# Delta-rule inverses on packed 32x32 diagonal blocks, masks in one operation, out projection begun on the other branches' rows

## The reference

```python
lower = jnp.where(strict, jnp.einsum('bhncd,bhnsd->bhncs', kb, k) * decay, 0.0)
eye = jnp.eye(cs, dtype=jnp.float32)
tinv = lax.linalg.triangular_solve(lower + eye, jnp.broadcast_to(eye, lower.shape),
                                   left_side=True, lower=True, unit_diagonal=True)
...
mix = jnp.concatenate([y_a, y_b, y_c], axis=-1) @ p['w_out'][l]
x = x + g1 * mix
```

## Time and profile before

| | us |
|---|---|
| median of 3 runs (2239.47 to 2243.78) | 2240.41 |
| profiled execution | 2252.45 |
| its span | 2250.3 |

### The profile page before, as it was taken

One profiled execution on the slowest core, in us unless ns is written; L12 is line 12 of the kernel. 1 busy time (PEld: TensorE's weight loads), 2 busy tenths in 40 slices (PEclk: granted clock), 3 DMA queues, 4 the chain that ended last, 5 costly groups with the idle time before them and its releaser, 6 DMA issues.

```text
span 2250.3 us, 35703 instructions
## 1 busy us (share of the span) xinstructions
PE 2027.0 (90%) x13488; PEld 1770.6 (79%) x13488; DVE 1040.9 (46%) x1950; ACT 689.9 (31%) x1394; POOL 189.5 (8%) x246
## 2 busy tenths in 40 slices
PE   4999988989799999997999879998299999999993
PEld 3777776887699999996778768875289989989782
DVE  2297254551433323332795645513372753827534
ACT  2110323330422112213112333303252643626422
POOL 1000002430000000001000023300100000000001
PEclk8999887999899999998998889998699999999995
DMA  8444269101222222313331200020667868869673
GB/s 294 162 173 176 97 262 420 67 21 60 70 84 92 84 68 84 102 58 120 129 131 50 75 1 1 8 73 0 233 189 240 315 203 286 280 229 326 190 252 126
DMA packets 87062, 328.10 MB, mean 146 GB/s; under 512 B 9666, under 2 KB 10274, under 8 KB 85634
## 3 DMA queue, kind: packets, MB, share of 16 engines
q1 hardware_dynamic: 78850, 295.17, 37.9%
q0 software_dynamic: 5120, 20.43, 2.4%
q10 hardware_dynamic: 2944, 10.49, 1.3%
HBM read 276.59 MB, written 49.46 MB: 145 GB/s over the span
## 4 chain that ended last, share of the span: by engine, by line
PE 85%; DVE 6%; DMA 3%; ACT 3%; issue 2%; POOL 1%; SPq 0%; ACTq 0%; POOLq 0%; DVEq 0%
PE PB L964 11%; PE PB L965 11%; PE PB L781 9%; PE PB L783 9%; PE PB L782 9%; PE PB L919 7%; PE PB L916 6%; PE PB L917 3%; PE PB L596 3%; PE PB L434 2%; PE PB L612 2%; PE PB L611 2%; PE PB L522 1%; PE PB L1015 1%; PE PB L957 1%
## 5 line engine op out<-in xcount | busy, mean ns | idle before, releaser
L964 PE MATMUL PB<-hT,ring 128*128 128x288 f32 x1024 | 343.2, 418 | 22.2 <-DVE hT L2020 12.2
L965 PE MATMUL PB<-hT,ring 128*128 128x288 f32 x1024 | 338.6, 413 | 0.0
L964 PEld LDWEIGHTS PB<-hT,ring 128*128 128x128 f32 x1024 | 196.6, 195 | 78.8 <-issue 19.8
L965 PEld LDWEIGHTS PB<-hT,ring 128*128 128x128 f32 x1024 | 198.9, 194 | 56.0
L781 PE MATMUL PB<-HH,VH 128*128 128x288 f32 x704 | 209.8, 298 | 17.2 <-DVE HL L1774 15.9
L916 PE MATMUL PB<-XX,UH 128*128 128x512 f32 (+3 forms) x704 | 213.0, 370 | 1.8 <-DVEq L1866 1.5
L782 PE MATMUL PB<-HL,VH 128*128 128x288 f32 x704 | 208.9, 297 | 0.0
L783 PE MATMUL PB<-HH,VL 128*128 128x288 f32 x704 | 208.2, 296 | 0.0
L917 PE MATMUL PB<-XX,UL 128*128 128x256 f32 (+3 forms) x704 | 181.6, 258 | 0.0
L781 PEld LDWEIGHTS PB<-HH,VH 128*128 128x128 f32 x704 | 133.2, 189 | 17.8 <-issue 17.8
L916 PEld LDWEIGHTS PB<-XX,UH 128*128 128x128 f32 x704 | 132.1, 188 | 13.3 <-DVEq L1866 1.9
(11 more groups left out here) (435 smaller groups left out, 3712.6 us busy)
## 6 DMA issues: line engine op xcount, KB each, us to landing
SS<-in_w_ada SPq DMA_DIRECT2D x88, 512.0 KB, 5.7
ring<-in_moe_gu SPq DMA_DIRECT2D x88, 512.0 KB, 4.6
RX<-in_moe_gu SPq DMA_DIRECT2D x88, 512.0 KB, 4.6
ring<-in_w_in SPq DMA_DIRECT2D x48, 512.0 KB, 3.5
ring<-in_ffn_gu SPq DMA_DIRECT2D x46, 512.0 KB, 3.4
RX<-in_moe_dn SPq DMA_DIRECT2D x44, 512.0 KB, 4.5
ring<-in_moe_dn SPq DMA_DIRECT2D x44, 512.0 KB, 4.5
moe_in<-CO SPq DMA_DIRECT2D x1, 15360.0 KB, 49.8
```

Of the source, the lines that this page charges most:

```text
L964: mm(PM[b][:, 0:HN], w, hT[:, k, 0:HN], start=(k == 0), stop=(k == KD - 1))
L965: end = mm(PS[b][:, 0:HN], w, hT[:, k, HN:T], start=(k == 0), stop=(k == KD - 1))
```

## The change

The five levels within blocks of 32 are done on the diagonal 32x32 blocks alone. ScalarE packs the four diagonal blocks of `UU` into `UC` (`diagonal_blocks`), VectorE masks them for all levels in one operation (`all_masks`), and GpSimd's `level_mask` is gone. `power` and `merged` issue 32x32 products, block `j` on rows and columns 32j of TensorE's array, for four heads after one wait; the three sets of chunks have a PSUM bank each. Level 5 joins blocks of 32 and level 6 those of 64, through full matrices `T64` and `TF` that GpSimd clears beforehand and into which ScalarE spreads the small blocks (`level_blocks`). The normalisation of chunks 0, 1 and 4 is shared out over later levels, and their turns move to level 5, level 6 and the tail. The first two tiles of the out projection are begun on rows 0, 1, 6 and 7 of `hT` in the tail, and finished on rows 2 to 5 where the projection stood. Two helper semaphores and eight small copies at the program's start, which cut the masks to 32 columns, complete it.

```diff
+Q = 32
+QLEVELS = 5
...
+        TC = [a.rearrange("p (a h c) -> p a h c", a=2, h=H) for a in (wk(7)[:, 0:256], wk(9)[:, 0:256], xaf[:, 640:896])]
...
+        LVQ = CO[:, C_LVL + QLEVELS * P:C_LVL + QLEVELS * P + QLEVELS * Q].rearrange("p (v c) -> p v c", c=Q)
+        IDQ = CO[:, C_LVL + QLEVELS * P + QLEVELS * Q:C_LVL + QLEVELS * P + (QLEVELS + 1) * Q]
+        quad = lambda j: slice(j * Q, (j + 1) * Q)
...
-        BANK_P, BANK_T, BANK_SM = (6, 4), (7, 0), (3, 2)
+        BANK_INV, BANK_SM = (6, 7, 5), (3, 2)
...
             def power(n, v):
...
+                m, b = chunk(n)[1], buf(n)
                 if v == 0:
...
+                    pe.wait_ge(S["um_ready"], prep(l, n))
                 else:
...
+                    pe.wait_ge(S["t_done"], inv(l, n, v - 1) + 1)
+                if v < QLEVELS:
+                    for hh in range(H):
+                        for j in range(m // Q):
+                            end = mm(p_out(n)[quad(j), hh, :], UM[b][quad(j), v, hh, :], IDQ[quad(j), :] if v == 0 else TC[b][quad(j), 0, hh, :],
+                                     start=True, stop=True, tile_position=(j * Q, j * Q))
+                elif v == QLEVELS:
+                    for hh in range(H):
+                        for j in (0, 2):
+                            end = mm(p_out(n)[quad(j + 1), hh, :], UU[b][quad(j), hh, (j + 1) * Q:(j + 2) * Q], TC[b][quad(j), 0, hh, :],
+                                     start=True, stop=True, tile_position=(j * Q, (j + 1) * Q))
+                else:
+                    pe.wait_ge(S["t64_ready"], full(l, n) + 1)
+                    for hh in range(H):
+                        end = mm(p64_out(n)[:, hh, :], UU[b][0:P // 2, hh, P // 2:P], T64[b][0:P // 2, hh, :],
+                                 start=True, stop=True, tile_position=(0, P // 2))
+                end.then_inc(S["p_pe"], 1)
             def merged(n, v):
...
+                m, b = chunk(n)[1], buf(n)
+                pe.wait_ge(S["p_copied"], merge(l, n, v) + 1)
+                t, pc = TC[b], PD[b]
+                for hh in range(H):
+                    if v < QLEVELS:
+                        for j in range(m // Q):
+                            mm(t_out(n)[quad(j), 0, hh, :], t[quad(j), 1, hh, :], pc[quad(j), hh, :], start=True, stop=True, tile_position=(j * Q, j * Q))
+                            end = mm(t_out(n)[quad(j), 1, hh, :], pc[quad(j), hh, :], t[quad(j), 1, hh, :], start=True, stop=True, tile_position=(j * Q, j * Q))
+                    elif v == QLEVELS:
+                        mm(t_out(n)[quad(1), 0, hh, :], t[quad(1), 1, hh, :], pc[quad(1), hh, :], start=True, stop=True, tile_position=(Q, Q))
+                        for j in (0, 2):
+                            end = mm(t_out(n)[quad(j), 1, hh, :], pc[quad(j + 1), hh, :], t[quad(j + 1), 1, hh, :],
+                                     start=True, stop=True, tile_position=((j + 1) * Q, j * Q))
+                    else:
+                        end = mm(t64_out(n)[:, hh, :], PC64[b][P // 2:P, hh, :], TF[b][P // 2:P, hh, P // 2:P], start=True, stop=True, tile_position=(P // 2, 0))
+                end.then_inc(S["t_pe"], 1)
             def t_final(n, last):
-                pe.wait_ge(S["t_done"], 2 * inv(l, n, last) + 2)
+                pe.wait_ge(S["t_done"], inv(l, n, last) + 1)
...
-                    end = mm(bank4(2, m)[:, hh, :], inv_tt(n, hh)[0:m, 0:m], VB[buf(n)][0:m, hh, :], start=True, stop=True)
+                    if n == 4:
+                        for j in range(m // Q):
+                            end = mm(out[quad(j), hh, :], TC[b][quad(j), 1, hh, :], v[quad(j), hh, :], start=True, stop=True, tile_position=(j * Q, j * Q))
+                    else:
+                        end = mm(out[:, hh, :], TF[b][:, hh, :], v[:, hh, :], start=True, stop=True)
...
-                if v == 2:
+                if v == 5:
                     back_to_features(0)
-                if v == 3:
+                if v == 6:
                     pe.wait_ge(S["yb_ready"], normed(l, 0))
                     back_to_features(1)
-                if v == 4:
-                    pe.wait_ge(S["yb_ready"], normed(l, 1))
-                    back_to_features(4)
...
             k_state(3)
+            pe.wait_ge(S["yb_ready"], normed(l, 1))
+            back_to_features(4)
             pe.wait_ge(S["r_ready"], stated(l, 3))
             t_final(3, LEVELS - 1)
             pe.wait_ge(S["vn_copied"], scan(l, 2))
...
             outputs(3, 0)
             new_state(3)
             outputs(3, 1)
+            pe.wait_ge(S["ya_ready"], 2 * (l + 1))
+            pe.wait_ge(S["yc_ready"], 2 * (l + 1))
+            pe.wait_ge(S["t_done"], len(INV) * (l + 1))
+            out_begun(0)
             pe.wait_ge(S["yb_ready"], normed(l, 4))
             back_to_features(2)
+            pe.wait_ge(S["o_copied"], NCH * (l + 1))
+            out_begun(1)
             pe.wait_ge(S["yb_ready"], normed(l, 2))
             back_to_features(3)
...
+            def out_part(l, s, rows):
+                for k in rows:
+                    w = ring[:, slot_of(FILL["out", l], s), k * P:(k + 1) * P]
+                    mm(PM[s][:, 0:HN], w, hT[:, k, 0:HN], start=(k == OTHER[0]), stop=(k == DELTA[-1]))
+                    end = mm(PS[s][:, 0:HN], w, hT[:, k, HN:T], start=(k == OTHER[0]), stop=(k == DELTA[-1]))
+                return end
...
+                if stage == "out":
+                    for s in range(2):
+                        out_part(l, s, DELTA).then_inc(S["w_used"], 1)
+                    for s in range(2, 4):
+                        wait_landed(pe, f0, s, 0)
+                        wait_free(s % 2, (t0 + s) // 2)
+                        tile_mms(slot_of(f0, s), s % 2)
...
+                def out_begun(s):
+                    wait_landed(pe, FILL["out", l], s, 0)
+                    wait_free(s, (TILE["out", l] + s) // 2)
+                    out_part(l, s, OTHER)
+                mixer_pe(pe, l, z_tile, out_begun)
...
+            def diagonal_blocks(n):
+                act.wait_ge(S["uu_ready"], prep(l, n))
+                for j in range(chunk(n)[1] // Q):
+                    e = fn(UC[buf(n)][quad(j)], UU[buf(n)][quad(j), :, j * Q:(j + 1) * Q], ACT.Copy)
+                e.then_inc(S["uuc_ready"], 1)
+            def level_blocks(n):
+                b = buf(n)
+                act.wait_ge(S["pad_ready"], 4 * l + 1)
+                act.wait_ge(S["t_done"], inv(l, n, QLEVELS - 1) + 1)
+                for j in range(P // Q):
+                    c = slice(j * Q, (j + 1) * Q)
+                    if j < 2:
+                        fn(T64[b][quad(j), :, c], TC[b][quad(j), 0], ACT.Copy)
+                    e = fn(TF[b][quad(j), :, c], TC[b][quad(j), 1], ACT.Copy)
+                e.then_inc(S["t64_ready"], 1)
             def copy_powers(n, v):
                 m = chunk(n)[1]
...
+                act.wait_ge(S["p_pe"], inv(l, n, v) + 1)
+                if v <= QLEVELS:
+                    fn(PD[buf(n)][0:m], p_out(n)[0:m], ACT.Copy).then_inc(S["p_copied"], 1)
+                else:
+                    fn(PC64[buf(n)][P // 2:P], p64_out(n), ACT.Copy).then_inc(S["p_copied"], 1)
...
+                diagonal_blocks(n)
             for g, grp in enumerate(GROUPS):
                 for v in range(LEVELS):
                     for n in grp:
                         if 0 < v < chunk(n)[2]:
                             copy_powers(n, v)
+                    if v == QLEVELS:
+                        for n in grp[0:2]:
+                            level_blocks(n)
                     if g == 0 and v == 5:
                         copy_v(4)
                     if g == 0 and v == 6:
                         copy_o(4)
-                    if g == 1 and v == 0:
-                        act.wait_ge(S["dd_ready"], prep(l, 3))
-                        squares_of(0)
-                        squares_of(1)
-                        squares_of(4)
-                    if g == 1 and v == 1:
+                    if g == 1 and v < 3:
+                        if v == 0:
+                            act.wait_ge(S["dd_ready"], prep(l, 3))
+                        squares_of(NORMED[v])
+                    if g == 1 and v == 3:
                         for n in (0, 1, 4):
                             root_of(n)
-                    if g == 1 and v in (2, 3, 4):
-                        normal(NORMED[v - 2])
+                    if g == 1 and v >= 4:
+                        normal(NORMED[v - 4])
...
-                then(dve.tensor_tensor(uu, uu, bank4(5, m, m), ALU.mult))
-                dve.tensor_tensor(UM[buf(n)][0:m, :, 0:m], uu, lvl(0, m).unsqueeze(1).broadcast_to([m, H, m]), ALU.mult).then_inc(S["um_first"], 1)
+                dve.tensor_tensor(uu, uu, bank4(5, m, m), ALU.mult).then_inc(S["uu_ready"], 1)
...
+            def all_masks(n):
+                m = chunk(n)[1]
+                levels = min(chunk(n)[2], QLEVELS)
```

(51 more changed lines are left out.)

89 lines of the change are left out of this document (26 added, 63 removed).

## The result

The changed kernel takes 2214.2 us (median; 2208.9 to 2215.0) where the kernel before took 2242.1 beside it: a ratio of 0.9867, interval 0.9841 to 0.9893. It is 28 us faster by the medians and 30 us by the ratio. The forecast was 86 us faster, and 2214 lies outside the predicted range. The profiled execution took 2208.9 us, with a span of 2206.7 us; the one shown of before had a span of 2250.3 us. These two lie 43.5 us apart, more than the medians, so what is read from them carries some of the spread of single runs.

What follows compares the result with a forecast made beforehand. TensorE's own passes were taken to bound both inversion stretches, not waits between engines. Terms: 51 + 39 + 2 + 10 - 16 = 86 us off 2240.4, so 2154 us; own range 2122 to about 2180, with rival one 2122 to 2208.

Steps and rivals of the forecast that it cites:

- What a 32-wide pass costs: TensorE's 32x32 products in the inversion levels: 12 ns a pass, with the four diagonal tiles overlapping.
- rival one: Inversion levels: diagonal tiles don't overlap, a pass costs 29 ns; 35 us off, 2205 us; chance 19%.
- One level: Each of levels 1 to 4, two chunks: 2.8 us where there were 5.9; 3.4 with the samples.
- the prediction's own signs of being wrong: Levels over 5 us, granted clock of 0.5 between the levels, or preparation growing by over 3 us.
- First groups: Inverses of chunks 0, 1 and the samples: 30.4 us against 57.3 and 55 in layers 0 and 1; 51 off.
- Second groups: Inverses of chunks 2 and 3: 22.8 us against 42.8 and 42 in layers 0 and 1; 39 off.
- Clock: Low clock after the level-5 waits, 3.5 us each, and 1 more at the first group's start: 16 us lost.
- Rival two: The clock stays low in the sparse levels; 18 us off in all, 2222 us; chance 8%.
- Level 5: Joining 32-blocks: ScalarE's twelve spreading copies, 3.6 us, become the narrow place, ahead of the copy of the samples' values.
- Tail: Finishing the last chunk: sixteen out-projection products move before the last normalisation; 5 us a layer, 10 off.
- Preparation: Mask and copy work before the inverses: between 3 us lost and 3 won per layer, 1 taken; 2 off.
- The sum: All terms over both layers: 86 us off, from 2240.4 to 2154 us for the median.

Runs made afterwards that it cites:

- experiment 2: Changed kernel with every 32x32 merge product of levels 1 to 4 issued twice in a row: 2288.6 us, ratio 1.0193 to the kernel before.
- experiment 8: Kernel before, with the padding writes moved out of layer 0's mixer to beside the feed-forward's weight loads: 2246.7 us, ratio 1.0001.
- Experiment 1: Changed kernel with the padding writes moved out of layer 0's mixer, in 60 pieces beside the feed-forward's weight loads: 2193.7 us, ratio 0.9771 to the kernel before.
- experiment 7: Changed kernel with padding writes moved, transposed products on VectorE and the copy of chunk 4's new values first: 2152.2 us, ratio 0.9574 to the kernel before.
- Experiment 3: Changed kernel with transposed products (second of each merge, all of level 0) moved from TensorE to VectorE's transpose: 2171.6 us, ratio 0.9668 to the kernel before.
- Experiment 6: Changed kernel with ScalarE's copy of chunk 4's new values ahead of the spreading copies at level 5: 2201.8 us, ratio 0.9806 to the kernel before.
- experiment 4: Changed kernel with the out projection begun as before, after all turns back to features: 2223.8 us, ratio 0.9904 to the kernel before.
- experiment 10: Kernel of experiment 7 plus one unread 512-column product in each of levels 1 to 4 of all four groups: 2140.3 us, ratio 0.9515 to the kernel before.

## Why the prediction was right or wrong

**What a 32-wide pass costs: right.** 12 ns was taken, within 8 to 29. The power products of two chunks, 64 passes at full clock, the start of the merge behind them, and the windows that give the clock, here and where level 0 ran at the lower level (columns as above):

```profile
1331.63 0.75 PE L596 MATMUL PB<-PJ 32*32 32x32 f32 x64
1332.49 0.27 PE L618 MATMUL PB<-PJ 32*32 32x32 f32 x7
1331.50:1333.00 1.50, 1.39 (x118) 1.15 (x118) 0.00 (x0) 0.56 (x2) 1.14 (x3) 1.00 0.00 0
360.57:361.40 0.83, 0.82 (x61) 0.83 (x65) 0.72 (x3) 0.08 (x1) 0.00 (x0) 0.50 1.00 405
```

The 0.75 us, with the pipeline's end, are under 12 ns a pass; by the starts alone it is 8.9 ns at the upper clock level and 13.3 at the lower. So the diagonal tiles do overlap although the four of a head write one PSUM bank. The Trainium skill ("TensorEngine Tiling (Array Packing)", Restrictions and Gotchas) says that different row tiles cannot do so at the same time; for these four tiles the measurement decides against it. Passes 30 ns apart, near rival one's 29, exist in experiment 2, but at the lower clock level and with eight in a row on one tile.

**One level: the step that failed.** "192 passes at 12 ns" was priced as if the array were the only limit. I counted four times as many passes and never asked what brings them: 192 passes are 384 instructions, one and a half packets. An estimate from the packets' spacing is 5.3 us a level at the 3.5 us of layer 1 and 10.7 at the 7.1 of layer 0, against the forecast 2.8 and the 5.9 before. Level 3 of the first group, the same work in layer 0 and in layer 1, shows the step alone (columns as above):

```profile
395.33:401.73 6.40, 2.13 (x189) 1.91 (x188) 0.42 (x1) 0.56 (x2) 2.01 (x3) 0.95 0.71 284
1331.63:1334.25 2.62, 2.19 (x190) 1.97 (x190) 0.42 (x1) 0.56 (x2) 2.01 (x3) 1.00 0.00 0
```

In layer 1 no packet is waited for, and the level takes 2.6 us, as forecast. In layer 0 one gap of 3.9 us lies in it, and it takes 6.4. With a sample update each, levels 1 to 4 of the second groups took 3.7 to 7.8 us where 3.4 were forecast. Two of the prediction's own signs of being wrong came: levels over 5 us, and a clock near 0.5 between them. The Trainium skill ("Runtime: NRT & Kernel Launch", Instruction fetch mechanics) speaks of instruction blocks of 256, which the trace shows, and calls their cost mostly hidden, which agrees with experiment 8 for the 128-wide products of before (ratio 1.0001) and not with the 39.8 us of gaps here: the measurement decides. The view was at hand before the run: the page's third part lists 98 instruction packets.

**First groups: 51 us forecast, 5.8 measured.** Of the 45 us missing, 32.0 are gaps over 0.9 us (23.9 and 8.1). Experiment 1 took 18.6 us of them back by DMA traffic alone, and experiment 7 came to 31.4 and 32.6 against the forecast 30.4, though with fewer products on TensorE than the forecast counted.

**Second groups: 39 us forecast, 15.4 measured.** The gaps are 7.8 of the 24 us missing. Six of the eight sample updates lie in this stretch. Four were charged with 0.6 us each and the last two with nothing; they now run in the chain, mostly at the lower clock level. Rows of the update's products in layer 1's second group, of before (L662) and of the changed kernel (L681; count, busy us, mean ns of a pass, idle before):

```profile
L662 PE MATMUL PB<-UA,XA 64*128 64x128 f32 x25 | 3.8, 286 | 0.0
L662 PE MATMUL PB<-UA,PJ 64*128 64x128 f32 x24 | 3.5, 285 | 0.0
L681 PE MATMUL PB<-UA,XA 64*128 64x128 f32 x27 | 6.9, 429 | 0.0
L681 PE MATMUL PB<-UA,PJ 64*128 64x128 f32 x24 | 5.3, 387 | 0.0
```

**Clock: 16 us were charged, in the wrong place.** It was expected to fall for 3.5 us behind each wait. It fell for most of all four groups, at clocks of 0.55 to 0.66, even where TensorE was busy for 33 of 37 us. Rival two said so, with 8%, and its 2222 lies near the result, but by luck: it has no gaps at packet boundaries, which are 39.8 us. Of the two causes the clock looks the lesser one. Experiment 1, which changed no instruction of TensorE's, took 20 us off; the wide product in the changed kernel, which lifted the clock and shortened the gaps as well, took off 6 us by the medians and 11 by the ratios, whose intervals all but touch. Experiment 3's 43 us don't tell the two apart, because passes went with the instructions.

**Level 5: right in kind.** ScalarE's spreading copies stand in the chain for 3.3 us (3.6 forecast), and the sample products wait behind them for 2.7 and 3.1 us:

```profile
412.37 0.60 ACT UA L1210
412.96 0.04 issue
413.01 1.97 PE PB L715 x8
414.98 5.20 PE PB L697 x64
```

Experiment 6 shows that this wait was not needed.

**Tail: right, a little small.** 5 us a layer were forecast; 7.6 and 5.6 were measured, and 7.1 and 7.7 by experiment 4. In the timeline the out projection's products stand where the 3.6 us of idle were the earlier trace rows, from 11.6 us after chunk 2's new values (about 12 forecast), at full clock, with one gap of 0.9 us (under 2 forecast):

```profile
495.36 0.65 PE L1001 MATMUL PB<-hT,ring 128*128 128x288 f32 x2
...
499.24 0.60 PE L689 MATMUL PB<-CO,PJ 128*128 128x128 f32 x4
...
503.56 0.60 PE L689 MATMUL PB<-CO,PJ 128*128 128x128 f32 x4
505.05 0.72 PE L1001 MATMUL PB<-hT,ring 128*128 128x288 f32 x2 [0.89 <-issue]
```

**Preparation: wrong in sign, within its bounds.** It grew by 1.7 and 1.1 us where 1 us less was forecast. What of it is the ScalarE copies and what the wider mask was not tried apart.

**The sum.** The five stretches of both layers are 34 us shorter between the two profiles, not 86. The two inversion terms carry 69 us of shortfall; 39.8 us of these are gaps at packet boundaries. The rest is the low clock, for which 16 us had been charged apart, and what I counted as hidden; no run here splits it.

## What to carry to other kernels

When a change cuts wide operations into many narrow ones, count instructions beside passes: divide the instructions of the stretch by 256, multiply by the spacing of instruction packets (3.5 us alone in this trace, 7.1 beside a saturating transfer), and compare that with the array time. A gap on an engine that waits for nothing, with the same number of instructions between one and the next, is the mark of it. Where such a stretch can't be avoided, keep bulk transfers away from it, and give other engines whatever products only rearrange data.

## What the runs showed of the hardware

- TensorE was brought one 16 KB packet of 256 instructions per 3.5 to 3.9 us with the DMA engines otherwise idle and per 7.1 to 7.5 us while they moved 416 GB/s. A packet itself took 0.9 to 1.5 us, under the burst no more than without; there it started 4.6 to 5.1 us after TensorE had gone on, otherwise 1.1 to 1.9. TensorE went on 1.2 to 1.6 us after a packet had arrived.
- 32x32 passes in the four diagonal tiles started 8.9 ns apart at the upper clock level and 13.3 at the lower, all into one bank; 30 ns apart, at the lower level, where eight in a row went to one tile.
- The granted clock stood at 0.56 over 29.2 us in which TensorE's products kept it busy for 28.4 (experiment 7), and rose to 0.83 with one 512-column product more in each of four levels (experiment 10): a busy TensorE is no promise of the upper level.
- VectorE's transpose of sixteen 32x32 blocks, 128x128 in all, took 0.31 us.
